# Weight blocks interleaved in pairs, and dense products that read them with a column step of two

## What is computed

```python
qkv = h @ w_qkv                    # 1024 x 3072, layers 1 and 2
m   = o @ w_o                      # 1024 x 1024
u   = rms_norm(x) @ ffn_w_in       # 1024 x 5632
f   = (gelu(conv(gate)) * val) @ ffn_w_out    # 2816 x 1024
x   = x + sigmoid(rms_norm(x) @ ple_w_gate) * (p @ ple_w_proj)
# layer 3: h @ w_in, o @ w_out, relu(h @ w_ff1)**2 @ w_ff2
```

## Time and profile before

| | kernel before |
|---|---|
| median of three runs | 2222.01 us |
| lowest, highest | 2221.18, 2223.2 us |
| span of the profiled execution | 2221.5 us |
| TensorE matmuls busy | 2158.3 us (97%), 14078 instructions |
| weight loads busy | 1723.8 us (78%), 14078 instructions |
| VectorE busy | 1289.8 us (58%) |
| ScalarE busy | 907.8 us (41%) |
| GpSimd busy | 119.7 us (5%) |
| moved by DMA | 189.77 MB, 85 GB/s on average |

### The profile page before, as it was taken

How to read it: one execution, slowest core, us unless ns; L and a number is a source line. 1 busy time by engine, 2 the same in 40 slices (tenths; PEclk the granted TensorE clock), 3 DMA queues, 4 the chain that set the end, 5 groups by cost and what they waited for, 6 DMA issues and landing times. The chain is left out here.

```text
span 2221.5 us, 35739 instructions
## 1 busy us (share of the span) xinstructions
PE 2158.3 (97%) x14078; PEld 1723.8 (78%) x14078; DVE 1289.8 (58%) x1733; ACT 907.8 (41%) x1421; POOL 119.7 (5%) x96
## 2 busy tenths in 40 slices
PE   8999999999999999999999998999898899999999
PEld 6777788888877777778888876777787566888887
DVE  5564576663378877476665347686456566333333
ACT  4444532222365666642222244654322545323321
POOL 0000011110000000001110000000333000000000
PEclk9999999999999999999999999999999999999999
DMA  7332233333324221323333331322000112333321
GB/s 255 105 107 65 76 113 96 94 98 101 94 75 134 91 66 47 105 74 106 95 100 99 94 95 50 100 85 76 3 4 4 47 39 64 107 94 102 97 94 66
DMA packets 54087, 189.77 MB, mean 85 GB/s; under 512 B 5968, under 2 KB 6224, under 8 KB 53840
## 3 DMA queue, kind: packets, MB, share of 16 engines
q1 hardware_dynamic: 53680, 187.49, 27.3%
q10 hardware_dynamic: 288, 0.59, 0.1%
HBM read 184.91 MB, written 3.15 MB: 85 GB/s over the span
## 5 line engine op out<-in xcount | busy, mean ns | idle before, releaser
L299 PE MATMUL l_banks<-l_r_hi,l_w_hi 128*128 128x512 f32 x1440 | 574.3, 399 | 3.5 <-DVE l_r_lo L1796 2.3
L301 PE MATMUL l_banks<-l_r_hi,l_w_lo 128*128 128x512 f32 x1440 | 561.0, 390 | 0.0
L300 PE MATMUL l_banks<-l_r_lo,l_w_hi 128*128 128x512 f32 x1440 | 560.8, 389 | 0.0
L284 DVE TENSOR_TENSOR l_w_lo<-ring,l_w_hi 128x1024 fp32r<-128x1024 f32 x216 | 299.0, 1386 | 96.0 <-ACT l_w_hi L278 92.3
L278 ACT ACTIVATE l_w_hi<-ring 128x1024 fp32r<-128x1024 f32 x216 | 227.1, 1056 | 293.8 <-PE l_banks L301 288.9
L299 PEld LDWEIGHTS l_banks<-l_r_hi,l_w_hi 128*128 128x128 f32 x1440 | 270.3, 188 | 72.7 <-issue 8.2
L300 PEld LDWEIGHTS l_banks<-l_r_lo,l_w_hi 128*128 128x128 f32 x1440 | 270.5, 188 | 57.6 <-issue 4.3
L301 PEld LDWEIGHTS l_banks<-l_r_hi,l_w_lo 128*128 128x128 f32 x1440 | 270.3, 188 | 57.0
L299 PE MATMUL ff_banks<-ff_r_hi,ff_w_hi 128*128 128x512 f32 x512 | 200.0, 391 | 0.0
L301 PE MATMUL ff_banks<-ff_r_hi,ff_w_lo 128*128 128x512 f32 x512 | 199.2, 389 | 0.0
L300 PE MATMUL ff_banks<-ff_r_lo,ff_w_hi 128*128 128x512 f32 x512 | 199.2, 389 | 0.0
(11 more groups left out here) (513 smaller groups left out, 3256.9 us busy)
## 6 DMA issues: line engine op xcount, KB each, us to landing
ring<-weights SPq DMA_DIRECT2D x315, 512.0 KB, 3.6
na_bias<-window_bias SPq DMA_DIRECT2D x16, 512.0 KB, 5.4
da_rel<-t_rel SPq DMA_DIRECT2D x8, 448.0 KB, 4.2
outT<-X SPq DMA_DIRECT2D x12, 256.0 KB, 2.1
X<-xT SPq DMA_DIRECT2D x8, 256.0 KB, 5.7
const<-consts SPq DMA_DIRECT2D x1, 1312.0 KB, 11.5
l_pt<-pT SPq DMA_DIRECT2D x2, 512.0 KB, 4.6
X<-outT SPq DMA_DIRECT2D x4, 256.0 KB, 3.2
```

The source lines that it names most:

```text
L284: dve.tensor_tensor(self.w_lo[:, c % self.slots, :], k.ring[:, g % RING, :], self.w_hi[:, c % self.slots, :].bitcast(F32), ALU.subtract).t ...
L299: pe.matmul(psum, hi, self.hi(rhs_slot), start=start, stop=False)
L300: pe.matmul(psum, hi, self.lo(rhs_slot), start=False, stop=False)
L301: return pe.matmul(psum, lo, self.hi(rhs_slot), start=False, stop=stop)
```

## The change

The host interleaves the two blocks of each pair. Of blocks 0 and 1 of a chunk, column 0 of block 0 now comes first, then column 0 of block 1, column 1 of block 0, and so on over 256 columns; then blocks 2 and 3, and so on. `multiply` names a block accordingly: every second column of the pair's 256 columns, starting at 0 for an even block and at 1 for an odd one. Its weights are therefore still 128 columns, now with a step of 2 elements (8 bytes) and spread over 1024 bytes of a partition in place of 512. Number, order and kind of all instructions, all waits and all sizes stay as they are, as do the values that meet in each product.

```diff
     def multiply(self, pe, psum, c, block, rhs_slot, start, stop):
 
-        cols = slice(block * P, block * P + P)
+        at = block // 2 * 2 * P + block % 2
+        cols = slice(at, at + 2 * P - 1, 2)
         hi, lo = self.w_hi[:, c % self.slots, cols], self.w_lo[:, c % self.slots, cols]
         pe.matmul(psum, hi, self.hi(rhs_slot), start=start, stop=False)
         pe.matmul(psum, hi, self.lo(rhs_slot), start=False, stop=False)
@@
     weights = np.concatenate(stream)
     assert weights.shape == (N_CHUNKS, P, BLK * P)
+    weights = weights.reshape(N_CHUNKS, P, BLK // 2, 2, P).transpose(0, 1, 2, 4, 3).reshape(N_CHUNKS, P, BLK * P)
```

## The result

| | before | changed |
|---|---|---|
| median | 2222.52 us (4 runs) | 2262.47 us (4 runs) |
| lowest, highest | 2221.18, 2223.2 us | 2262.04, 2264.1 us |
| span of the profiled execution | 2221.5 us | 2260.9 us |

A forecast was written before the change was run, and what follows sets the result against it. The prediction took TensorE's dense matmul pace as the bound. Its terms, all 0 on the 2221.5 us span, plus about 0.5 us outside it, gave 2222 us (no change, chance 0.34), range 2136 to 2326 us.

The forecast's parts named there:

- What bounds the kernel: Whole kernel: TensorE sets the end through 7560 dense matmuls at 226.7 ns, 1714 us or 77% of the span.
- the leverage of 7.56 us for each ns: Dense matmuls on TensorE: one nanosecond of pace is worth 7.56 us, 0.34%.
- The host's layout at nothing: Transfer, rounding and subtraction of each chunk: the host's interleaving costs the device 0.
- The length of a load: Weight loads on TensorE: about 28 ns for fp32r, 109 ns plain; twice or fourfold length stays hidden, 0 in steady stream.
- The cover: Dense stream on TensorE: time that hides an fp32r load behind the running matmul, about 199 ns.
- The bound for exposed loads: Loads after idle TensorE, about 93 places: at most 2.6 us at 28 ns each, 7.5 us at 81 ns.
- What the load takes from the stream, costed at 0: Stepped load beside the running dense matmul: takes nothing more than now, 0; rivals range from -10 to +13 ns per matmul.
- the 13.4 ns: Dense pace above 213.3 ns for 512 columns; taken as a fixed cost of changing weights, indifferent to addresses.
- The prediction's own last sign: If layer 1's attention moves otherwise than the feed-forward parts, relative address decides and the forecast's argument is wrong.
- Stealing by lines: Dense stream: load takes read slots by lines touched, +13.3 ns per matmul, +100.5 us, 2322 us; chance 0.21.
- The faster one: Dense stream: the step takes the load off the stream, -10.1 ns per matmul, 2142 us or part way; chance 0.30.
- The phase is worse, by less: Dense matmuls outside layer 1's attention: new addresses bring its 233 ns pace, +46 us, 2268 us; chance 0.13.

The follow-up runs named there:

- e7: Kernel before plus an unused tile shifting activations against weights by 64 bytes (layers 1, 2), 128 (layer 3 mixer input), 192 (layer 3 feed-forward): 2242.76 us.
- e10: Kernel before plus an unused tile shifting activations against weights by 32 bytes (layers 1, 2), 256 (layer 3 mixer input), 224 (layer 3 feed-forward): 2258.32 us.
- e6: Kernel before; loads in layers 1 and 2 name one column 128 times, layer 3 feed-forward's second matmul loads and computes 64 of 128 columns: 2239.3 us.
- e3: Against the kernel before: four blocks interleaved by the host, weights read with a step of four elements: 2284.6 us, ratio 1.0274.
- e4: Against the kernel before: all eight blocks of a chunk interleaved, weights read with a step of eight elements: 2349.46 us, ratio 1.0565.
- e9: Changed kernel plus an unused tile shifting activations against weights by 64 bytes (layers 1, 2), 128 (layer 3 mixer input), 192 (layer 3 feed-forward): 2262.53 us.

## Why the prediction failed, by its own steps

**What bounds the kernel.** Right. TensorE's dense pace decides; the other engines and the transfers were unmoved; the leverage of 7.56 us for each ns holds (+44.2 us for 7560 matmuls, 5.8 ns on average).

**The host's layout at nothing.** Right, 0.9995 (0.9985 to 1.0006).

**The length of a load.** The reading was wrong, though its conclusion held. I took 28 ns from the distance of the load and the matmul of the first L299 behind plain products. That is not the load's length: the matmul ahead of it was still streaming, and the recorded start of a matmul lies ahead of its own work. At an idle array a first matmul is recorded 1 to 2 ns behind its load, and starts 0.34 us ahead of the next matmul, not 0.23. From load to load at such a place it is 109 ns, like the plain ones, so the sign that the prediction saw of a faster load for fp32r (28 against 109 ns) is gone. The cover is then 227 - 109 = 118 ns, not 199. By these lengths the 7 ns that a step of two adds are covered, and the 104 ns of a step of four just so. The bound for exposed loads, 2.6 to 7.5 us, was too high for this step: 7 ns at 93 places are 0.7 us.

**What the load takes from the stream, costed at 0.** This step failed: it measured +5.8 ns for each matmul, 44 us. The reason given was that the 13.4 ns are the same in the feed-forward parts of three layers, hence indifferent to addresses. But these parts all have the same relative address of weights and activations modulo 256 bytes. Layers 1 and 2 even share the tiles. They were one case seen three times, and the one stage with another address, layer 1's attention at 233 ns, stood in the earlier trace rows and contradicted it. The prediction's own last sign came true: that attention did not move, while the feed-forward parts did. e7 and e10 show the dependence: a shift alone moves the same loads between 226.67 and 233.33 ns. e6 shows the other half: the 13.4 ns are no fixed cost either.

**The rivals.** Stealing by lines (2322 us) falls with e3, e4 and e6. The faster one (2142 us) falls too: no edit in any kernel brought a feed-forward part below 226.67 ns. "The phase is worse, by less" was nearly right in size and in its picture: a second resting point 6.6 ns up, taken by the matmuls outside of layer 1's attention, +46 us and 2268 us, while that attention stays as it was. Measured: layer 1's attention nearly unmoved (233.3 ns before, 232.8 after), one grid step of 6.67 ns up in layers 1 and 3, +44.2 us in all, less the 4.8 us that shorter waits and transitions gave back. (It counted all 576 dense matmuls of that attention as slow; by the kernel only the 432 on `na_more` are shifted. That is worth 1 us.) Its name for the cause, new addresses, is only half shown: the step acts like a shift in that the two don't add (e9), but no shift tried undoes it. It had 0.13, and the forecast 0.34: with a row of the trace beside it that had the very pace, it deserved more.

**The waits behind the pace.** Their giving back 4.8 us was missing in the sum.

**Two rules beside it.** The Trainium skill, SBUF — State Buffer, "Door 1: The DMA port swizzle", has two accesses to a 16-byte line as enough. For the length of a load alone the runs nearly agree: 109, 116 and 211 to 213 ns for four, two and one access. By that rule the time would have stayed at 2222 us, and the measurement says 2262: a load that is hidden is not thereby free. The Trainium skill, TensorE: Matmul & The Clock Gate, "Step-by-step: what each phase is for", has the load and the stream on ports that don't disturb each other. The measured pace depends on their relative address and on the step of the load, so in these runs they do.

**Still open.** What repeats every 6.667 ns; why a load that is 7 ns longer, or one that spans twice the addresses, comes to rest one unit higher; and whether the length or the spread of the load does it. Few columns (e6) and the shifts (e7, e10) show that addresses can move the pace at an unchanged length of 108 to 109 ns, so the length isn't needed for such a move. For the steps of two, four and eight no run separates the two, since each step changes both.

## What to carry to other kernels

When a stream of matmuls runs back to back, its pace can be a resting point between the weight load and the moving columns, and anything that changes either (a step, a relative address, even fewer columns) may move it by several ns: measure the pace from start to start in each stage before and after. In these runs contiguous fp32r weights at the same offset as the activations modulo 256 bytes had the best pace of all that was tried; a stage whose pace differs from the others' at the same shapes is worth a look at its addresses. And when a number looks the same everywhere, ask what else is the same in all those places before calling it a fixed cost.

## What the hardware showed that was not expected

The steady patterns are whole multiples of 6.667 ns, 34 to 881 of them, in every feed-forward part whose pattern repeats within 24 matmuls; layers 2 and 3 with a step of eight showed no such short pattern. Leaving out 4 of 512 moving columns made one stage 9 ns a matmul slower (235.55 against 226.67 ns) and left the next, with the same code, at 226.67. A load that names one column 128 times was as long alone as one of 128 columns (108 to 109 ns) and made the stream slower (228.89 and 231.11 against 226.67 ns). A step of four makes a load about twice as long (109 to 212 ns) but the stream only 8.3 ns slower, while a step of eight, with a load of nearly the same length (214 to 216 ns), costs 18.1 ns.
